# Prompt attention of a two-layer decoder: scores two steps ahead, in halves between the two heads' transposes

## The reference

```python
def blk(args):
    qb, qib, wb, pos = args
    sc = indexer_scores(qib, wb, k_idx)
    sc = jnp.where((key_pos[None, :] <= pos[:, None])[None], sc, -jnp.inf)
    _, idx = lax.top_k(sc, topk)
    valid = idx <= pos[None, :, None]
    return sparse_attend(qb, _gather_rows(k, idx), _gather_rows(v, idx), valid)
```

## Time and profile before

| | |
|---|---|
| median of 3 runs | 3243.0 us |
| all three | 3237.93, 3243.0, 3244.01 us |
| profiled execution: first to last instruction (span) | 3218.5 us |
| TensorE busy | 3014.0 us (94%) |
| VectorE busy | 1604.0 us (50%) |
| ScalarE busy | 1334.5 us (41%) |
| GpSimd busy | 262.7 us (8%) |

### The profile page before, as it was taken

How to read it: one execution, slowest core, us unless ns; L and a number is a source line. 1 busy time by engine, 2 the same in 40 slices (tenths; PEclk the granted TensorE clock), 3 DMA queues, 4 the chain that set the end, 5 groups by cost and what they waited for, 6 DMA issues and landing times.

```text
span 3218.5 us, 56238 instructions
## 1 busy us (share of the span) xinstructions
PE 3014.0 (94%) x20185; PEld 2635.5 (82%) x20185; DVE 1604.0 (50%) x3493; ACT 1334.5 (41%) x2398; POOL 262.7 (8%) x334
## 2 busy tenths in 40 slices
PE   7999878889999999999989997889899999999998
PEld 5899433558999999999989963346599999999998
DVE  4565699764722322322556567986474222222234
ACT  4433688665522122122443247866564211211234
POOL 1012321011000000000000141100300000000000
PEclk8999989989999999999999998999899999999999
DMA  6622365026311111111432343620642111111124
GB/s 201 163 65 69 108 236 184 2 100 196 99 52 43 48 46 43 48 46 46 116 89 55 69 131 132 209 92 2 230 129 63 45 46 50 46 42 52 46 72 139
DMA packets 356491, 293.60 MB, mean 91 GB/s; under 512 B 85288, under 2 KB 319206, under 8 KB 356024
## 3 DMA queue, kind: packets, MB, share of 16 engines
q1 hardware_dynamic: 325036, 186.21, 19.8%
q0 software_dynamic: 31152, 104.76, 10.5%
q10 hardware_dynamic: 108, 0.11, 0.0%
HBM read 273.33 MB, written 9.78 MB: 88 GB/s over the span
## 4 chain that ended last, share of the span: by engine, by line
PE 64%; DVE 6%; issue 3%; ACT 2%; DMA 1%; POOL 0%; DVEq 0%; ACTq 0%; POOLq 0%; SPq 0%
PE bank L859 44%; PE bank L876 11%; PE bank L843 2%; DVE arena L2635 2%; PE bank L1436 1%; PE bank L1410 1%; DMA arena<-in_cache_v,page_idx 1%; PE bank L917 1%; ACT arena L1902 1%; DVE w_lo L2107 1%; PE bank L1241 0%; PE bank L1370 0%; PE bank L1499 0%; POOL arena L725 0%; ACT w_hi L1629 0%
## 5 line engine op out<-in xcount | busy, mean ns | idle before, releaser
L859 PE MATMUL bank<-h_hi,w_hi 128*128 128x352 f32 x2736 | 891.7, 326 | 11.7 <-DVE arena L2261 7.2
L859 PE MATMUL bank<-h_lo,w_hi 128*128 128x352 f32 x2736 | 880.0, 322 | 0.0
L859 PE MATMUL bank<-h_hi,w_lo 128*128 128x352 f32 x2736 | 879.2, 321 | 0.0
L2107 DVE TENSOR_TENSOR w_lo<-weights,w_hi 128x1024 fp32r<-128x1024 f32 x250 | 306.4, 1225 | 678.0 <-ACT w_hi L1629 671.5
L859 PEld LDWEIGHTS bank<-h_hi,w_hi 128*128 128x128 f32 x2736 | 515.9, 189 | 17.2 <-issue 13.7
L859 PEld LDWEIGHTS bank<-h_lo,w_hi 128*128 128x128 f32 x2736 | 516.5, 189 | 0.3
L859 PEld LDWEIGHTS bank<-h_hi,w_lo 128*128 128x128 f32 x2736 | 515.2, 188 | 0.0
L1629 ACT ACTIVATE w_hi<-weights 128x1024 fp32r<-128x1024 f32 x250 | 264.1, 1056 | 453.3 <-PE bank L859 294.6
L843 PEld LDWEIGHTS bank<-arena 128*128 128x128 f32 (+2 forms) x1717 | 199.3, 148 | 163.3 <-issue 95.3
L843 PE MATMUL bank<-arena 128*128 128x128 f32 (+2 forms) x1717 | 271.1, 290 | 46.1 <-ACT arena L1939 15.8
L876 PE MATMUL bank<-g_hi,w_hi 128*128 128x352 f32 (+2 forms) x768 | 255.7, 333 | 11.1 <-DVE arena L767 5.4
(11 more groups left out here) (396 smaller groups left out, 4369.6 us busy)
## 6 DMA issues: line engine op xcount, KB each, us to landing
arena<-in_w_ada SPq DMA_DIRECT2D x96, 512.0 KB, 4.5
weights<-in_w_down SPq DMA_DIRECT2D x48, 512.0 KB, 3.9
weights<-in_w_gate SPq DMA_DIRECT2D x44, 512.0 KB, 3.8
weights<-in_w_up SPq DMA_DIRECT2D x44, 512.0 KB, 3.8
weights<-in_w_in SPq DMA_DIRECT2D x66, 256.0 KB, 3.8
weights<-in_w_down SPq DMA_DIRECT2D x32, 448.0 KB, 3.6
weights<-in_w_out SPq DMA_DIRECT2D x96, 128.0 KB, 2.9
weights<-in_w_out SPq DMA_DIRECT2D x48, 256.0 KB, 3.1
```

Of the source, the lines that this page charges most:

```text
L859: mm = pe.matmul(bank[:, 0:TC], wt[:, w], xt[:, x], start=(k + m == 0), stop=(k == n_k - 1 and m == 2))
L2107: dve.tensor_tensor(w_lo[:, w], S(O_W + n % 2 * UNIT, UNIT), w_hi[:, w].bitcast(F32), ALU.subtract).then_inc(unit_lo, 1)
```

## The change

Scores are made two steps ahead. PE's order in step p becomes: transposes of head 0, `scales` if due, the first piece of `qk(p + 2)`, transposes of head 1, the second piece of `qk(p + 2)`, `pv(p - 1)`, `mask`. DVE's order becomes `scales`, the first piece of `logits(p + 2)`, `turned(p)`, its second piece, `reciprocals`, `heads`, selection. ACT alternates by head: copies of head 0's transposes, `probs(p + 1)` of head 0, the copy of head 1's, `probs(p + 1)` of head 1, then `negated`. Selection 1 is made before step 0, between the masks of steps 0 and 1, and every later piece one step sooner. The exponentials get a third buffer, and work space of the selection moves to make room.

```diff
-SEL_STEP = {0: ((1, 0), (1, 1)), 1: ((1, 2), (1, 3))}
+SEL_STEP = {}
 for _m in range(2, 7):
     for _k in range(4):
-        SEL_STEP[4 * _m - 6 + _k] = ((_m, _k),)
+        SEL_STEP[4 * _m - 7 + _k] = ((_m, _k),)
...
-        O_EQ, O_CUM, O_GT, O_EQS = (R(5 + n) for n in range(4))
+        O_EQ, O_CUM, O_CUMS, O_GT, O_EQS = H(0), H(1), R(6), R(7), R(8)
...
-        O_PB = [[R(14, 1024 * (2 * t + g)) for g in range(2)] for t in range(2)]
+        O_PB = [[R(14, 1024 * (2 * t + g)) for g in range(2)] for t in range(2)] + [[R(5, 1024 * g) for g in range(2)]]
+
+        def probs_at(p, g):
+
+            return R(14, 1024 * (2 + g) + 512) if p > 15 and p % 3 == 2 else O_PB[p % 3][g]
+
...
-                def qk(p):
+                def qk(p, part):
                     b, i, done = PAIRS[p]
-                    for c0 in range(0, P * (b + 1), 512):
+                    for c0 in range(512 * part, P * (b + 1), 512)[:1]:
...
-                def turns(p):
+                def turns(p, g):
                     b, i, done = PAIRS[p]
-                    for g in range(2):
-                        pe.wait_ge(probs_ready, l * 64 + 2 * p + g + 1)
-                        for k0 in range(0, b + 1, 4):
-                            ring = Dr if g and k0 else A
...
+                    pe.wait_ge(probs_ready, l * 64 + 2 * p + g + 1)
+                    for k0 in range(0, b + 1, 4):
+                        ring = Dr if g and k0 else A
...
-                qk(0)
+                for p in range(2):
+                    for part in range(2):
+                        qk(p, part)
                 for p in range(32):
-                    if p < 31:
-                        qk(p + 1)
+                    turns(p, 0)
                     if p % 4 == 1 and p > 4:
                         scales(p // 4 - 1)
-                    turns(p)
+                    if p < 30:
+                        qk(p + 2, 0)
+                    turns(p, 1)
+                    if p < 30:
+                        qk(p + 2, 1)
                     if p:
                         pv(p - 1)
...
                 A.use(AB_FEW)
-                probs(0)
+                for g in range(2):
+                    probs(0, g)
                 for p in range(32):
-                    if p % 4 == 2 and p < 24:
+                    for g in range(2):
+                        turned(p, g)
+                        if p < 31:
+                            probs(p + 1, g)
+                    if p % 4 == 1 and p < 24:
                         negated(p // 4 + 1)
-                    turned(p)
-                    if p < 31:
-                        probs(p + 1)
...
-                def logits(p):
+                def logits(p, part):
...
-                    for g in range(2):
-                        dve.tensor_reduce(S(M_NMX + 2 * (p % 2) + g, 1), S(M_MX + 4 * (p % 2) + 2 * g, k), AX.X, ALU.max, negate=True).then_inc(logits_ready, 1)
+                    for g in range(2 if part == k - 1 else 0):
+                        dve.tensor_reduce(S(M_NMX + 2 * (p % 3) + g, 1), S(M_MX + 4 * (p % 3) + 2 * g, k), AX.X, ALU.max, negate=True).then_inc(logits_ready, 1)
...
-                logits(0)
+                logits(0, 0)
+                logits(0, 1)
+                select(1, 0)
+                select(1, 1)
+                logits(1, 0)
+                logits(1, 1)
+                select(1, 2)
+                select(1, 3)
                 for p in range(32):
-                    if p < 31:
-                        logits(p + 1)
+                    if p % 4 == 1 and p > 4:
+                        scales(p // 4 - 1)
+                    if p < 30:
+                        logits(p + 2, 0)
+                    turned(p)
+                    if p < 30:
+                        logits(p + 2, 1)
                     if p % 4 == 0 and p:
                         reciprocals(p // 4 - 1)
-                    if p % 4 == 1 and p > 4:
-                        scales(p // 4 - 1)
-                    turned(p)
```

More of the change, by code:

```diff
@@ L782, in build @@
         O_HIST, O_REJ, O_ABOVE = O_SMALL + 12, R(9), R(9, 128)
-        M_MX, M_NMX, M_SUM, M_RS, M_SMX = (O_SMALL + i for i in (148, 156, 12, 28, 36))
+        M_MX, M_NMX, M_SUM, M_RS, M_SMX = (O_SMALL + i for i in (148, 160, 12, 28, 36))
         ACR, XDT, BTK = ((R(2), R(2, 512)), (R(8, 512), R(8, 768)), (R(10, 256), R(10, 384)))
@@ L1412, in _ @@
                 turned = {}
-                def turns(p):
+                def turns(p, g):
                     b, i, done = PAIRS[p]
-                    for g in range(2):
-                        pe.wait_ge(probs_ready, l * 64 + 2 * p + g + 1)
-                        for k0 in range(0, b + 1, 4):
-                            ring = Dr if g and k0 else A
[L1420 to L1423, removed]
+                    pe.wait_ge(probs_ready, l * 64 + 2 * p + g + 1)
+                    for k0 in range(0, b + 1, 4):
+                        ring = Dr if g and k0 else A
+                        bank = ring.open()
+                        for k in range(k0, min(k0 + 4, b + 1)):
+                            mm = T(B(bank, [[1, P]], P * (k - k0)), S(probs_at(p, g) + P * k, P))
+                        ring.close(mm)
                     turned[p] = A.count.n, Dr.count.n
@@ L1916, in negated @@
                         return
-                    step.only(act.activation(neg_s[:, 1024:1024 + NS], S(O_CUM + 1024, NS), ACT.Copy, bias=-BIG, scale=BIG))
-                    step(act.activation(neg_s[:, 0:1024].rearrange("q (r p) -> q r p", r=RUN), S(O_CUM, 1024).rearrange("q (p r) -> q r p", r=RUN),
+                    step.only(act.activation(neg_s[:, 1024:1024 + NS], S(O_CUMS + 1024, NS), ACT.Copy, bias=-BIG, scale=BIG))
+                    step(act.activation(neg_s[:, 0:1024].rearrange("q (r p) -> q r p", r=RUN), S(O_CUMS, 1024).rearrange("q (p r) -> q r p", r=RUN),
                                         ACT.Copy, bias=-BIG, scale=BIG))
@@ L2763, in _ @@
                 step(dve.tensor_copy(S(O_M1 + P, P), C("causal")))
-                def logits(p):
+                def logits(p, part):
                     b, i, done = PAIRS[p]
                     full = P * (b + 1)
-                    if i == 0 and b > 1:
+                    if i == 0 and b > 1 and part == 0:
                         dve.wait_ge(neg_ready, l * 7 + NB - b)
-                    for c, c0 in enumerate(range(0, full, 512)):
+                    for c, c0 in list(enumerate(range(0, full, 512)))[part:part + 1]:
                         w = min(512, full - c0)
@@ L2775, in logits @@
                             settle(dve)
-                            Dr.done(dve.tensor_tensor_reduce(out=S(O_PB[p % 2][g] + c0, w), in0=bank[:, 0:w], in1=mask, scale=HD ** -0.5, scalar=-3e38,
-                                                             op0=ALU.add, op1=ALU.max, accum_out=S(M_MX + 4 * (p % 2) + 2 * g + c, 1)), wait=(c0 + w == full))
+                            Dr.done(dve.tensor_tensor_reduce(out=S(probs_at(p, g) + c0, w), in0=bank[:, 0:w], in1=mask, scale=HD ** -0.5, scalar=-3e38,
+                                                             op0=ALU.add, op1=ALU.max, accum_out=S(M_MX + 4 * (p % 3) + 2 * g + c, 1)), wait=(c0 + w == full))
                     k = (full + 511) // 512
-                    for g in range(2):
-                        dve.tensor_reduce(S(M_NMX + 2 * (p % 2) + g, 1), S(M_MX + 4 * (p % 2) + 2 * g, k), AX.X, ALU.max, negate=True).then_inc(logits_ready, 1)
+                    for g in range(2 if part == k - 1 else 0):
+                        dve.tensor_reduce(S(M_NMX + 2 * (p % 3) + g, 1), S(M_MX + 4 * (p % 3) + 2 * g, k), AX.X, ALU.max, negate=True).then_inc(logits_ready, 1)
                 def turned(p):
```

23 lines of the change are left out of this document (11 added, 12 removed).

## The result

| | before | after |
|---|---|---|
| median, 20 runs each | 3244.41 us | 3254.59 us |
| lowest to highest | 3237.65 to 3256.30 | 3236.70 to 3264.78 |
| ratio, 95% interval | | 1.0026, 1.0015 to 1.0038 |
| first profiled execution, span | 3218.5 us | 3244.2 us (the run: 3246.49) |
| TensorE busy | 3014.0 us | 3034.6 us |

The change makes the kernel slower by 0.15 to 0.38%. The forecast of no change, 3242 us with a range up to 3252, was wrong. The last column also corrects a number of the text ahead: only 2.3 us lie around a span (3246.49 less 3244.2). By that, the first profile of before, 3218.5, was an execution 17 us faster than any of the timed runs (3237.65 less 2.3 is 3235.4); the experiments show what it lacked.

What follows compares the result with a forecast made beforehand. TensorE (PE), with least room, bounds the kernel. Per layer reordering 0, waits -4.3, opening +2.3; two layers -4.0, clock +3.4, total -0.6 on a 3218.5 us span, plus 24.5 around it: 3242 us, range 3231 to 3252.

Steps and rivals of the forecast that it cites:

- Halves: Blocks 7 to 4: one head's transposes take 0.69 to 1.03 us, with ACT's copy wait covered by scores.
- second pieces: Wide steps: the second score piece waits 0 to 0.30 us for DVE to read its bank, +2.2 a layer.
- Opening: Stage's start: DVE's earlier selection delays the second value products by 4.2 us, net +2.3 a layer.
- the clock: Each opening: PE's idling brings 3.4 us of half clock, costing 1.7 a layer, +3.4 in all.
- theory O: Theory tested in the experiments: the stage's opening costs more than the wide steps give back.
- The terms for the wide steps: Blocks 7 to 4, per layer: reordered halves and scores save 4.1 us, the new bank wait costs 2.2.
- the scale products and exponentials: PE's waits at scale products (1.7) and behind exponentials (2.6) go with two steps of lead: -4.3 a layer.
- the first short steps: Part of blocks 3 to 0, whose 16 steps each pay 0.11 us for splitting the heads' transposes, +1.8 a layer.
- the sum without its clock: Both layers' stages: reordering 0, waits -4.3 and opening +2.3 make -2.0 a layer, -4.0 for two.
- the slower one: Wide steps: four banks hold PE to DVE's pace; with 0.4 us more a step 3253 us; chance 0.22.
- Switches free: Changes of work on PE cost nothing, removing 6.2 us a layer of counted cost: 3230 us; chance 0.03.
- hidden anyway: After the stage: the gathers' transfers, not their release, set the end, so nothing changes: 3243 us; chance 0.04.

Runs made afterwards that it cites:

- before_look: The kernel before, without edits, profiled and timed once more: 3251.57 us, ratio 1.0001 to the kernel before.
- after_look: The changed kernel, without edits, profiled and timed once more: 3257.60 us, ratio 1.0031 to the kernel before.
- fill_open: The changed kernel plus 24 unread transposes of a constant where PE stands in the opening: 3246.62 us, ratio 1.0006 to the kernel before.
- lead_half: The changed kernel with one and a half steps of lead, reciprocals first, heads together in blocks 3 to 0: 3231.77 us, ratio 0.9956 to the kernel before.
- small_again: The changed kernel with both heads' transposes together in blocks 3 to 0, second measurement: 3256.27 us, ratio 1.0017 to the kernel before.
- before_hold: The kernel before with the first gathers of values held until the last scores are masked: 3256.94 us, ratio 1.0026 to the kernel before.

## Why the prediction was wrong

Point by point, for a layer, from the profiles of before_look and after_look (layer 0 unless named):

- Halves, no wait for the copy, second pieces 2.05 us after the first ones: right, as shown above.
- Opening: 4.2 for DVE's order and 1.7 for the clock, together 5.9 to the second value products. Measured 5.5 (27.54 less 22.06); by fill_open 1.7 of it is the clock. Right, and with the next point theory O falls.
- From there to the value products of step 19, 84.4 us against 90.5: a gain of 6.1. The terms for the wide steps (-4.1 + 2.2), the scale products and exponentials (-4.3) and the first short steps (some 0.4) make 5.8. Right.
- A wait that I had removed came back elsewhere: the scale products of step 21 were moved ahead of the scores, and the reciprocals that they need stand behind DVE's masks. The step takes 5.6 for 3.7 us. I had written that the reciprocals stand a step earlier and not asked when DVE gets to them.
- From the value products of step 20 to those of 24, beside the gathers: 18.7 against 16.9, 1.8 lost. The sum had nothing for this.
- From step 24 to the last value products: 12.3 at full clock or 19.6 at half (layer 1), against 16.2 and 14.2. Before_look's layers take 148.3 in the mean; so a layer of the changed kernel takes 0.2 more if the clock comes back (148.5), and 7.6 more if not (156.0).

**The step that failed is the clock, at the stage's end.** The sum counted half clock in the opening alone (1.7 a layer) and left the end as the earlier trace rows had it. Those rows are from an execution that the timed runs are not like: the prediction put 24.5 us around its span as launch and end, and only 2.3 us lie there. What it lacked is PE standing beside the gathers, and just there the change adds: a step of 8.4 to 10.1 us for 6.1 to 7.8, and then 20 us or more of half clock at a stretch in 8 of 16 layers of the kernels with two steps of lead. In before, before_look and the two kernels with one and a half steps it is in none of 8; I don't know what decides it. In those 8 layers it takes 18.5 to 19.6 us from the value products of step 24 to the last ones, in every other layer of the kernels with more lead 11.8 to 13.1. That makes some 6 us for each long stretch, and about one a run. The Trainium skill's page "TensorE: Matmul & The Clock Gate", section "What's actually happening", has it that an idle engine falls to half and steady work brings full clock back. The first half agrees with the rows; the second doesn't cover 20.5 us at 0.50 with PE recorded busy for 19.94.

The timed runs agree. In the runs of the kernel before, time rises by 0.31 us for each us of half clock (35 runs, scatter about the line 2.6 us); the two go together, which doesn't by itself show the one as the cause of the other. At 230 us of it, that line gives 3247.3 for before and 3249.3 for after_look by its own line. Of the 8 us between their means (3259.5 and 3251.3), 19 us more half clock x 0.31 makes 6. The sum had 6.8 of the 19. So by this line the clock isn't the whole of it: at the same half clock 2.0 us are left, where the sum without its clock had -4.0. By the layers above it nearly is (0.2 against 7.6). How much goes to the two waits that the sum put at nothing, the reciprocals' 1.9 and the 1.8 beside the gathers in each layer, these runs don't decide.

Of the rivals, the slower one named the right size (3253) for a wrong reason: the four banks held PE by no more than was counted. "Switches free" and "hidden anyway" fell; what the stage's end loses does go through. The POOL queue was released by the first weighting at 743.15 instead of 727.13, of which 4 us lay ahead of the stage (571.0 for 567.1). And of the experiments without a hold, lead_half, with the shortest stages (287.3 us for both by the table), has the shortest span, 3233.8, and small_again, with the longest (308.6), the longest, 3267.2.

## What to carry to other kernels

When a profiled span lies below every timed run, look first for what that one execution lacked; here it lacked PE's stands beside the gathers, where the case was decided. A change that makes an engine's own order tighter should be costed at the place where DMA traffic stops it, and for the clock that it finds afterwards, not only where its steps run freely. Lead costs an opening: with half a step less of it the second value products came 2.2 us later than before instead of 5.5, and that kernel, which differs in other points too, was the fastest.

## What the runs showed of the hardware

While indirect gathers moved 248 to 346 GB/s, results of PE reached ACT and DVE microseconds after their recorded ends (4.15 us above, at 696.50 of before_look); held gathers took this out of the stage in all four layers, and it then stood beside them later (5.78 us of idle DVE before 720.24 in before_hold). In the first profile of before, with up to 389 GB/s, there was none of it. Why the results come late is open. After such a stand the same work ran on at half clock for 6.8 us in one layer and 44 in another of the same execution (after_look, from 699.9 and from 2283.7). And 24 transposes that nothing reads were cheaper than letting PE stand: the second value products came at 25.9 us with them, at 27.5 without.
